# One buffer for the gathered tokens, and expert weights by halves over 21 places

## What is computed

```python
x = x + hierarchical_moe(rms_norm(x, norm_ffn), ...)     # 32 experts, each token goes to 2 of one group of 8
x = rms_norm(x, norm_final)
# the second block starts: q, k, v = split(rms_norm(x) @ attn_w_qkv_2), ...

def expert_rows(xb, e):                       # for each expert e, on the tokens that chose it
    g = xb @ w_gate[e]                        # 1024 -> 512
    u = xb @ w_up[e]                          # 1024 -> 512
    return (silu(g) * u) @ w_down[e]          # 512 -> 1024
```

## Time and profile before

| | us |
|---|---|
| median of 3 runs | 964.09 (963.83 to 966.66) |
| profiled execution | 965.7 |
| its span | 964.5 |
| TensorE busy | 927.3 of it (96%) |
| VectorE busy | 455.5 (47%) |
| ScalarE busy | 356.7 (36%) |
| read from HBM | 290 MB, 302 GB/s over the span |

### The profile page before, as it was taken

How to read it: one execution, slowest core, us unless ns; L and a number is a source line. 1 busy time by engine, 2 the same in 40 slices (tenths; PEclk the granted TensorE clock), 3 DMA queues, 4 the chain that set the end, 5 groups by cost and what they waited for, 6 DMA issues and landing times.

```text
span 964.5 us, 12359 instructions
## 1 busy us (share of the span) xinstructions
PE 927.3 (96%) x4961; PEld 614.3 (64%) x4961; DVE 455.5 (47%) x775; ACT 356.7 (37%) x577; POOL 24.6 (3%) x41
## 2 busy tenths in 40 slices
PE   7999999999999999999999999887999989999997
PEld 6979889885444443444434433333999878888886
DVE  5878665445232322313222222213776667776444
ACT  7634555432221121221212211115654456665332
POOL 1400000000000000000000000000000000000000
PEclk9989999999999999999999999999999999999999
DMA  9954454596999999999999999999844535555401
GB/s 371 395 217 150 172 175 158 232 378 265 399 427 429 424 430 427 425 429 427 428 428 426 429 425 427 427 431 418 337 141 165 180 130 192 177 190 200 174 1 45
DMA packets 30685, 291.88 MB, mean 303 GB/s; under 512 B 5025, under 2 KB 5665, under 8 KB 7714
## 3 DMA queue, kind: packets, MB, share of 16 engines
q1 hardware_dynamic: 30194, 290.89, 74.8%
q10 hardware_dynamic: 432, 0.17, 0.1%
HBM read 290.00 MB, written 1.05 MB: 302 GB/s over the span
## 4 chain that ended last, share of the span: by engine, by line
PE 83%; DMA 10%; DVE 4%; ACT 1%; issue 1%; POOL 0%; SPq 0%; DVEq 0%; ACTq 0%
PE bank L1644 19%; PE bank L451 11%; PE bank L452 11%; PE bank L453 11%; PE bank L1666 10%; PE bank L2196 6%; DMA ring<-in_w_gate_up_second 5%; DMA ring<-in_w_gate_up_first 4%; PE bank L1616 3%; PE bank L2198 3%; PE bank L1682 3%; DVE w_low L547 1%; DMA head<-in_head 1%; PE bank L768 1%; PE bank L815 1%
## 5 line engine op out<-in xcount | busy, mean ns | idle before, releaser
L547 DVE TENSOR_TENSOR w_low<-ring,w_high 128x2048 fp32r<-128x2048 f32 x76 | 173.9, 2290 | 90.7 <-ACT w_high L515 90.4
L1644 PE MATMUL bank<-ring,arena 128*64 128x512 f32 x928 | 206.9, 595 | 7.3 <-DMA ring<-in_w_gate_up_second 5.3
L515 ACT ACTIVATE w_high<-ring 128x2048 fp32r<-128x2048 f32 x76 | 145.5, 1916 | 128.2 <-PE bank L453 94.2
L1644 PEld LDWEIGHTS bank<-ring,arena 128*64 128x64 f32 x928 | 64.9, 137 | 134.4 <-issue 118.3
L1781 DVE SCALAR_TENSOR_TENSOR y_low<-bank,arena,y_high 64x512 fp32r<-64x512 f32 x64 | 48.0, 750 | 137.8 <-ACT y_high L1716 137.4
L1666 PE MATMUL bank<-ring,arena 128*64 128x512 f32 x464 | 106.0, 598 | 4.4 <-issue 4.4
L2196 PE MATMUL bank<-xT_low_high,w_high 128*128 128x512 f32 x256 | 90.6, 399 | 1.3 <-DVE xT_low_high L558 1.1
L1716 ACT ACTIVATE y_high<-bank,arena 64x512 fp32r<-64x512 f32 x64 | 43.7, 683 | 125.8 <-PE bank L1666 125.3
L1772 DVE TENSOR_TENSOR arena<-bank,arena 128x256 f32<-128x256 f32 x32 | 13.6, 425 | 147.3 <-ACT arena L1703 147.3
L1703 ACT ACTIVATE arena<-bank 128x256 f32<-128x256 f32 x32 | 12.3, 385 | 190.8 <-PE bank L1644 190.8
L2198 PE MATMUL bank<-xT_low_high,w_low 128*128 128x256 f32 x256 | 71.8, 280 | 0.0
(11 more groups left out here) (317 smaller groups left out, 1617.7 us busy)
## 6 DMA issues: line engine op xcount, KB each, us to landing
ring<-in_w_down SPq DMA_DIRECT2D x28, 2048.0 KB, 27.5
ring<-in_w_gate_up_first SPq DMA_DIRECT2D x27, 2048.0 KB, 23.7
ring<-in_w_gate_up_second SPq DMA_DIRECT2D x27, 2048.0 KB, 25.2
ring<-in_dense_second SPq DMA_DIRECT2D x48, 1024.0 KB, 4.8
ring<-in_dense_first SPq DMA_DIRECT2D x28, 1024.0 KB, 6.2
extra_piece<-in_w_down SPq DMA_DIRECT2D x3, 2048.0 KB, 22.3
extra_piece<-in_w_gate_up_first SPq DMA_DIRECT2D x3, 2048.0 KB, 26.4
extra_piece<-in_w_gate_up_second SPq DMA_DIRECT2D x3, 2048.0 KB, 32.0
```

Source lines behind the costliest of these rows:

```text
L515: SC.activation(parts[buffer[0][u]][0][:, :], lanes[n % len(lanes)], ACT.Copy).then_inc(*high.inc(u))
L547: DVE.tensor_tensor(p[1][:, :], lanes[n % len(lanes)], p[0][:, :].bitcast(F32), ALU.subtract).then_inc(*split.inc(u))
L1644: last = PE.matmul(GU[t * SLOTS:(t + 1) * SLOTS, 0:NGU], xs[:, k, :], wgu[:, :, c, t * (DE // JT):(t + 1) * (DE // JT)], start=k == 0, sto ...
```

## The change

- The gathered tokens have one buffer, `GATHERED` in `arena[2]`, in two layouts in turn. In one the words lie by piece and then by expert, in the other by expert and then by piece, so that piece p of the next four is written exactly where the tokens of expert p of the present four were. The write therefore waits until that expert's gate and up are done (`n + 1` in place of `FOUR * four`). In ScalarE's step the write of an even piece moves from before silu to after the copy of the hidden rows.
- `arena[0]` becomes a 21st place of 1 MB for weights; the ten places become twenty of 1 MB. Its first load, the first half of expert 3's second piece, is issued at the end of `first_sync` after the last reads of X.
- The tenth early piece is now expert 3's first piece and not its down piece; the ten early pieces stay whole.
- All other weights are loaded in halves of 1 MB in the order in which they are multiplied (`ORDER`), each half when the half 21 places earlier has been read. Gate and up go by quarters, down by halves, each with its own wait and signal.
- The eight units of the second block wait for single halves of experts 28 and 29; they go to slots 8, 0, 1, 2, and the buffers of the second block move to slots 3 to 7. `norm_final` is issued after all eight, and waits for expert 31's gate and up.
- Several counts of the second block use semaphores of the first again (no change in what waits for what).

```diff
-    XTE = [arena[i][:, 0:KC * FOUR * SLOTS].rearrange("p (c s) -> p c s", c=KC) for i in (2, 0)]
+    GATHERED = arena[2][:, :]
+    def gathered(layout, p, experts):
+        if layout == 0:
+            block = GATHERED[:, p * 512:(p + 1) * 512].rearrange("p (e c s) -> p c e s", e=FOUR, c=2)
+        else:
+            block = GATHERED.rearrange("p (e q c s) -> p q c e s", e=FOUR, q=NPIECES, c=2)[:, p, :, :, :]
+        return block[:, :, 0:experts, :]
...
-        early_piece(RING, w_down, 3, unit1.at("om2"))
+        early_piece(RING, w_first, 3, unit1.at("om2"))
         early_piece(5, w_down, 2, unit1.at("om3"))
+        SP.wait_ge(rows_summed, 1)
+        SP.wait_ge(*rows_low_done.at(1))
+        SP.dma_start(place_words(PLACES - 1), w_second[3][:, 0:UNIT]).then_inc(place_sem[PLACES - 1], 16)
...
+    def gate_up_quarters(n, quarters_):
+        for j in quarters_:
+            PE.wait_ge(*landed(n, j))
+            gate_up(q, n, place_words(place_of(n, j)), n // FOUR % 2, n % FOUR, j, read_signal(n, j))
+
+    def down(n):
+        for j in (4, 5):
+            PE.wait_ge(*landed(n, j))
+            down_half(q, n, place_words(place_of(n, j)), n % 2, j - 4, read_signal(n, j))
...
     def scalar_step(n):
         four, pair = n // FOUR, n // 2
+        silu_out(q, n)
+        hiddenT_out(q, n)
         for p in pieces_at(n):
             if p % 2 == 0:
-                xT_even_out(q, four + 1, p, (four + 1) % 2, FOUR * four)
-        silu_out(q, n)
-        hiddenT_out(q, n)
+                xT_even_out(q, four + 1, p, (four + 1) % 2, n + 1)
...
-            SP.wait_ge(*q.at("down", n - 3))
-            load_piece(first, w_first[n], place_sem[first])
-            SP.wait_ge(*q.at("gate_up_first", n - 2))
-            load_piece(second, w_second[n], place_sem[second])
-            SP.wait_ge(*q.at("gate_up", n - 2))
-            load_piece(dn, w_down[n], place_sem[dn])
+    def expert_load(n, j):
+        SP.wait_ge(*has_read(*ORDER[ORDER.index((n, j)) - PLACES]))
+        src, half = ((w_first, w_second, w_down)[j // 2][n], j % 2)
+        place = place_of(n, j)
+        SP.dma_start(place_words(place), src[:, half * UNIT:(half + 1) * UNIT]).then_inc(place_sem[place], 16)
...
-    SP.wait_ge(*q.at("down", NE - 3))
-    for u in order2[0:2]:
+    for u, read in zip(order2[0:8], ORDER[ORDER.index((NE - 4, 4)):]):
+        SP.wait_ge(*has_read(*read))
         load_second(u)
-    SP.wait_ge(*q.at("gate_up_first", NE - 2))
-    for u in order2[2:4]:
-        load_second(u)
-    SP.wait_ge(*q.at("gate_up", NE - 1))
+    SP.wait_ge(*q.at("gate_up", NE))
     load_row("norm_final", a["norm_final"].rearrange("(l n) -> l n", l=1))
-    SP.wait_ge(*q.at("down", NE - 2))
-    for u in order2[4:6]:
-        load_second(u)
-    for u in order2[6:8]:
-        load_second(u)
```

More of the change, by code:

```diff
@@ L284, in build_program, with place_words @@
     w_down = a["w_down"]
+    def place_words(place):
+        if place == PLACES - 1:
+            return arena[0][:, :]
+        whole = ring if place < 2 * RING else extra
+        return whole[:, place % (2 * RING) * UNIT:(place % (2 * RING) + 1) * UNIT]
     loads = Loads(nc)
@@ L1635, in turn_route, with gate_up @@
         last.then_inc(*q.inc("turned"))
[L1637 to L1642, removed]
+    def gate_up(q, n, words, layout, e, quarter, signal):
+        w = words.rearrange("p (c m n) -> p m c n", c=2, m=2)
+        xs = gathered(layout, quarter, FOUR)[:, :, e, :]
+        for c in range(2):
+            k = 2 * quarter + c
             for t in range(JT):
-                last = PE.matmul(GU[t * SLOTS:(t + 1) * SLOTS, 0:NGU], xs[:, k, :],
-                                 wgu[:, :, c, t * (DE // JT):(t + 1) * (DE // JT)], start=k == 0, stop=k == KC - 1,
+                last = PE.matmul(GU[t * SLOTS:(t + 1) * SLOTS, 0:NGU], xs[:, c, :],
+                                 w[:, :, c, t * (DE // JT):(t + 1) * (DE // JT)], start=k == 0, stop=k == KC - 1,
                                  tile_position=(0, t * SLOTS), skip_group_check=True)
-        if KC // 2 - 1 in chunks_:
-            last.then_inc(*q.inc("gate_up" if half else "gate_up_first"))
-        return last
+        last.then_inc(*signal)
     def turn_hidden(q, n):
@@ L1656, in turn_hidden, with down_half @@
         last.then_inc(*q.inc("hidden_turned"))
[L1658 to L1663, removed]
+    def down_half(q, n, words, odd, half, signal):
+        if half == 0:
+            PE.wait_ge(*q.at("hiddenT", n + 1))
+            PE.wait_ge(*q.at("y", n))
+        wd = words.rearrange("p (c n) -> p c n", n=D)
+        for c in range(K4 // 2):
+            k = half * K4 // 2 + c
             o = (k % HCH) * P + (k // HCH) * SLOTS
@@ L1666, in down @@
                 last = PE.matmul(DN[t * SLOTS:(t + 1) * SLOTS, 0:NY], HT[:, o:o + SLOTS],
-                                 wd[:, k, (t ^ odd) * NY:((t ^ odd) + 1) * NY], start=k == 0, stop=k == K4 - 1,
+                                 wd[:, c, (t ^ odd) * NY:((t ^ odd) + 1) * NY], start=k == 0, stop=k == K4 - 1,
                                  tile_position=(0, t * SLOTS), skip_group_check=True)
-            if half_read and k == K4 // 2 - 1:
-                last.then_inc(half_read, 1)
-        last.then_inc(*q.inc("down"))
+        last.then_inc(*signal)
     def scatter(q, y_made, turned_, b, h, signal, mark=None, second_half_made=None):
@@ L1824, in tensor_step @@
     def tensor_step(n):
-        s, four, buffer, pair, odd = n % FOUR, n // FOUR, n // FOUR % 2, n // 2, n % 2
+        s, four, pair, odd = n % FOUR, n // FOUR, n // 2, n % 2
         b = pair % 3
-        first, second, dn = places_of(n)
-        value_first, value_second, value_dn = landed(n)
         for p in pieces_at(n):
@@ L1837, in tensor_step @@
         PE.wait_ge(*q.at("routeT", n + 1))
[L1838 to L1848 removed]
+        gate_up_quarters(n, range(4))
         for p in pieces_at(n):
@@ L1967, in tensor_begin @@
         PE.wait_ge(*q.at("xT_odd", 2))
-        gate_up(q, 0, second, 0, 0, 1, (2, 3))
+        gate_up_quarters(0, (3,))
         gather_even(q, 1, 0)
@@ L1972, in tensor_begin @@
         turn_route(q, 1, 0, 1, 1, GU)
-        PE.wait_ge(place_sem[dn], 16)
-        down(q, 0, piece(dn), 0, first_down_half)
+        down(0)
     def scalar_begin():
@@ L1997, in build_program @@
     vector_begin()
-    for n in range(3, NE):
-        expert_loads(n)
+    for n, j in ORDER[PLACES:]:
+        expert_load(n, j)
     for n in range(1, NE - 1):
```

193 lines of the change are left out of this document (80 added, 113 removed).

## The result

The changed kernel takes **977.31 us** (median of 4 runs, 975.66 to 978.70), beside 964.06 for the kernel before on the same chip (4 runs). The ratio on record is 1.0104, with an interval of 1.0081 to 1.0126: 10.0 us slower, 7.8 to 12.1. It is not the quotient of the two medians, which stand further apart, 13.3 us; two of the four runs of the changed kernel lie near 978.6 and two near 975.9. The forecast was 971.8, range 960.0 to 977.5: the side was right and the time lies in the range, but at its dear end. The profiled executions stand 10.3 us apart in their spans, 964.5 and 974.8, and the reading goes by these.

A forecast was written before the change was run, and what follows sets the result against it. Transfers were taken to bound the experts' stage; -2.45 + 3.9 + 4.3 + 2.0 = +7.75 us on the 964.09 median gave 971.8, range 960.0 to 977.5.

The forecast's parts named there:

- What bounds, and the tie: Experts' stage: transfers set its end; v0.0's round on ScalarE starts at 664.37, directly before expert 31's y_high.
- Part 1, the place: Weight stream near 226 to 232 us: the 21st place's early load fills the standing gap, -2.45 us, at most 5.5.
- rival C: Stream's start, 226 to 250 us: the extra transfer also removes the thin stretch, -5.5 us, giving 958.6; chance 0.20.
- Part 2, the halves' releases: Expert stream past 250 us: earlier releases give 0; a finer last step's 1.8 us is hidden by v0.0's round.
- Part 3, the rate: Experts' stream: 162 units in 8 KB rows run at 424 GB/s instead of 428, +3.9 us, bounds 0 to 7.6.
- Parts 4 and 5, SP's issues and the single buffer: Experts' stage: SP's 82 extra issues run beside the stream and later gathered writes hide under the down; 0 each.
- Part 6, the row: Second block: norm_final lands behind all eight units, VectorE waits 4.7 us, TensorE idles before q0, +4.3 us.
- Rival B: Second block: norm_final isn't waited for and the rate holds, so the unit alone counts, 961.6; chance 0.22.
- Part 7, the clock: TensorE at q0: its clock falls to 0.50 after the idle time, +2.0 us, bounds 0 to 3.4.

The follow-up runs named there:

- e4: The kernel before with each later whole piece loaded as two 1 MB column halves with 8 KB rows; 973.2 us, ratio 1.0063.
- e1: The changed kernel with norm_final issued after four of the eight second-block units again; 970.67 us, ratio 1.0035.
- e7: The changed kernel with norm_final after four units and the 21st place's first load issued only after expert 0's first quarter was read; 971.15 us, ratio 1.0042.
- e2: The changed kernel with norm_final after four units and ScalarE writing expert 31's y_high ahead of v0.0's round; 969.75 us in one run.
- e11: The changed kernel's single buffer and one unit ahead in arena[0], but whole transfers from expert 5 on and norm_final after four units; 969.53 us, ratio 1.0037.
- e3: The kernel before with only norm_final moved, issued after all eight second-block units; 973.07 us, ratio 1.0070.
- e12: The changed kernel itself, measured again in a later session; 974.72 us, ratio 1.0083.
- e8: The changed kernel with norm_final after four units and later halves in neighbouring places joined into 2 MB transfers; 965.71 us, ratio 0.9983.
- e9: The kernel before with each later piece as two 1 MB transfers, even and odd partitions, keeping 16 KB rows; 966.38 us in one run.
- e10: The kernel before with weights laid in HBM so each 2 MB transfer reads two unmergeable 8 KB runs per partition; 972.66 us in one run.
- e5: The kernel before with each later piece as two 1 MB transfers of 64 neighbouring partitions, keeping 16 KB rows; 1357.32 us in one run.
- e6: The kernel before with each later 2 MB transfer written as two 8 KB runs per partition, which were merged again; 970.0 us in one run.

## Why the prediction was right, and where it wasn't

**What bounds, and the tie** (right). The transfers set the end of the experts' stage, and v0.0's round came directly before y_high. T0 moved with the stream in every kernel that keeps this order.

**Part 1, the place** (-2.45 forecast; -2.4 in T0 - S0 of e4 against e1, -1.7 with the changed kernel's own trace, -2.7 by the ratios). The size was right, as far as these three can tell. The reason was half right: e7 shows that the gap needn't be filled, since the thin stretch behind it takes the unit as well. The ceiling of 5.5, with rival C on it, was never near: 332 GB/s in 234 to 250, not 428. With the row late C needed 9.2 us, more than its own ceiling, so it could turn the sign only with the row in time.

**Part 2, the halves' releases** (0 forecast). The sum was not hurt, but two sentences fall. No 1.8 us waited behind the round (e2). And "the next releases come where they came before" needs the halves: with whole transfers over the shifted places e11 starves at 260 to 300. The finer last step also had a price that I didn't name: TensorE ends expert 31 earlier and then stands 3.25 us before the scatter's first matmul (L1700, 1.55 us in e3), and in e1 the granted clock is 0.62 in 672 to 676 behind it. It cost e1 nothing that span - T0 shows (299.7 against 300.1). But the clock behind this stand differs between runs: it stayed 1.00 in the changed kernel's first trace and was 0.62 and 0.53 in 672 to 674 and 674 to 676 in e12, after the same 3.3 us. VectorE comes to z_gain at T0 + 14.5 in the first, as before, and at T0 + 15.0 to 15.6 in e1, e7, e8 and e12, where the clock fell.

**Part 3, the rate** (+3.9 forecast; 6.1 to 6.6). **This is the term that failed in size.** By its own formula 421 GB/s gives 162 x (2.491 - 2.450) = 6.6 us; T0 - S0 of e4 shows 6.6, its ratio 6.1. The step that failed is the choice of 424, "the purest of the rows": these are stretches of eight and fifteen us, and 400 us show 421. Why the short ones stood higher is open. The row of 420 that I took for an end of the range, because of the half-MB row in it, was the better one. The bound of 7.6 held. With 424 the same formula gives 162 x (2.473 - 2.450) = 3.7 us; the forecast's 3.9 comes of a 2.449 that 428 GB/s doesn't give. e9 and e10 give the cause that the prediction left in a pair ("rows of 8 KB and twice the transfers"): it is the rows. The Trainium skill, "DMA: Bandwidth & Descriptors", section "Why small descriptors are slow", has by the estimate above 0.6% for this; the measured 1.7% decides.

**Parts 4 and 5, SP's issues and the single buffer** (0, right as far as it shows). In the chain that ended last of the kernel after SP's issues have 4%, because SP is held when many transfers stand in the queue: it took 19.83 us for the eight units from 638.26, where a single issue took 0.33 elsewhere. The stream was full all that time. No run has the single buffer alone. It is in e8, which is no slower than the kernel before, so a cost of it beyond the place's gain isn't seen.

**Part 6, the row** (+4.3 forecast; 4.42). Landing at T0 + 19.3 for T0 + 19.2, VectorE's wait 4.80 for 4.7, TensorE's 4.42 for 4.3. That it fits to 0.1 us is luck in part: the surplus over the plain sum was T0 + 9.6 less 8.6, 1.0 us and not the 0.7 that was added. VectorE came to it at 682.67, T0 + 14.5, as forecast. In e12 the row landed at T0 + 19.2 again, but VectorE came at T0 + 15.4, so its wait was 3.75 and TensorE's 3.18; the clock that had fallen before it (Part 2) goes with that. Rival B, in which the row isn't waited for, is out.

**Part 7, the clock** (+2.0 forecast). The granted clock was lower behind the idle time, at its lower level or between the two. Busy time by stretch, kernel after:

```profile
690.00:692.00 2.00, 0.00 (x0) 0.00 (x0) 2.00 (x2) 2.00 (x3) 0.00 (x0) 0.66 0.60 137
692.00:694.00 2.00, 1.92 (x9) 1.92 (x10) 0.79 (x7) 1.34 (x2) 1.64 (x4) 0.50 0.98 264
694.00:696.00 2.00, 2.00 (x11) 2.00 (x11) 2.00 (x4) 1.65 (x2) 0.47 (x1) 0.50 0.98 397
696.00:698.00 2.00, 2.00 (x13) 2.00 (x12) 1.79 (x1) 0.00 (x0) 0.00 (x0) 0.63 1.03 434
698.00:700.00 2.00, 2.00 (x19) 2.00 (x18) 0.00 (x0) 0.00 (x0) 0.00 (x0) 1.00 0.63 188
```

The busy time by what the clock lacks, 1.92 x 0.5 + 2 x 0.5 + 2 x 0.37, is 2.7 us, inside the bounds. It is worked out from one trace.

**The sum.** With 6.6, 2.7 and 4.4 in their places: -2.4 + 6.6 + 4.4 + 2.7 = 11.3; the profiled pair shows 10.3, with an S0 that came 1.1 earlier, 11.4 without that, and the ratio says 10.0 (7.8 to 12.1). The forecast's 7.75 was short by 2.7 in the rate and 0.7 in the clock. What the median of four lies above this (977.3, where 964.1 + 11.3 is 975.4) has no trace of its own, and that 977.3 still lies under the range's end of 977.5 is luck.

**Left open.** The 0.7 us between T0 - S0 of the changed kernel and of e1, which load alike until the last units, was not pursued; e12 has 0.2. It wasn't tried what a place for the 21st unit brings with whole rows everywhere and releases in step.

## What to carry to other kernels

When a stage is bound by its transfers, splitting them along the row costs rate: here 8 KB rows moved 421 GB/s where 16 KB rows moved 428, and neither the number of the transfers nor their size, 1 or 2 MB, mattered. If a transfer must be halved, every other partition kept the rate and blocks of neighbouring partitions lost half of it. Take a rate from a long, pure stretch of steady state, or keep the worse row as the value. Of a small load that is moved in a queue in order, add up the bytes that now stand ahead of it and follow its one reader and what is queued behind that reader: here a row of 0.5 MB cost about as much as the rate did (6.9 and 6.6 us in the traces).

## What had not been expected of the hardware

**Half the rate for blocks of 64 partitions.** 221 GB/s with the DMA share at 1.01 (e5), against 428 for even and odd partitions (e9). The cause was not looked for.

**The length of the slow clock behind one idle stretch differs from run to run, and the whole kernel moves with it.** Around 51 us TensorE waits 1.8 to 2.0 us for VectorE in every kernel, and goes on between 51.8 and 52.9; the instructions of that stage are those of the kernel before. What differs is how long the clock is at its lower level afterwards. The first matmuls behind the wait, in the kernel after and in e4:

```profile
52.42 1.09 PE L762 MATMUL bank<-arena,ones 1*128 1x512 f32 x2 [1.78 <-DVE arena L1238]
...
52.39 1.98 PE L750 MATMUL bank<-arena,ones 1*128 1x512 f32 x2 [1.78 <-DVE arena L1226]
```

Busy time by stretch of the kernel after:

```profile
54.00:57.00 3.00, 3.00 (x15) 2.12 (x14) 2.38 (x7) 0.28 (x3) 0.00 (x0) 0.79 0.83 347
57.00:60.00 3.00, 3.00 (x11) 2.47 (x11) 1.90 (x5) 2.94 (x6) 0.00 (x0) 0.64 0.04 16
60.00:62.00 2.00, 2.00 (x10) 1.65 (x9) 2.00 (x2) 0.43 (x1) 0.00 (x0) 1.00 0.00 0
```

And of e4:

```profile
57.00:60.00 3.00, 3.00 (x10) 1.70 (x9) 1.93 (x5) 2.70 (x5) 0.00 (x0) 0.50 0.03 11
60.00:62.00 2.00, 2.00 (x7) 1.61 (x7) 2.00 (x2) 0.63 (x1) 0.00 (x0) 0.50 0.00 0
62.00:64.00 2.00, 2.00 (x9) 1.61 (x8) 1.90 (x4) 0.63 (x1) 0.00 (x0) 0.82 0.50 86
```

The mean clock of 50 to 64 took three values over all the kernels, and S0 goes with it: 0.88 and S0 at 230.9 to 231.5 (after, e3, e7, e8), 0.76 and 232.0 to 232.4 (before, e1, e2, e9, e12), 0.63 and 234.3 to 234.8 (e4, e6, e10, e11). T0 - S0 doesn't go with it, so these up to 3.9 us pass to the end of the kernel. They are probably a good part of the spread of the kernel before, 963.2 to 971.7 over its runs on all chips. There is a trace of only one of these runs, but their times go with the mean clock: 0.997 in the ten of 963.2 to 964.4, 0.990 to 0.992 in the seven of 969.9 to 971.7. The drift of S0 is also the reason why the kernels here are compared by S0 and T0 where there is one trace of each.
